# Running sums of the decay: one token-major copy in place of a second, head-major product

## What is computed

```python
a_cs = jnp.cumsum(a_dt, axis=-1)                       # per head, over the chunk's tokens
seg = a_cs[..., :, None] - a_cs[..., None, :]          # token t minus token s
decay = jnp.where(mask, jnp.exp(jnp.where(mask, seg, 0.0)), 0.0)
cb = jnp.einsum("bclgn,bcsgn->bcgls", cm, bm)
y_diag = jnp.einsum("bcgls,bcgrls,bcsgrp->bclgrp", cb, decay, xdt)
decay_to_end = jnp.exp(a_cs[..., -1:] - a_cs)
```

## Time and profile before

| | us |
|---|---|
| median of 3 runs | 2788.34 (2787.91 to 2789.7) |
| profiled execution, its own time | 2790.36 |
| span of that execution | 2788.5 |
| PE busy | 2737.2 |
| DVE busy | 1883.0 |
| ACT busy | 1454.7 |
| POOL busy | 818.0 |

### The profile page before, as it was taken

How to read it: one execution, slowest core, us unless ns; L and a number is a source line. 1 busy time by engine, 2 the same in 40 slices (tenths; PEclk the granted TensorE clock), 3 DMA queues, 4 the chain that set the end, 5 groups by cost and what they waited for, 6 DMA issues and landing times.

```text
span 2788.5 us, 38529 instructions
## 1 busy us (share of the span) xinstructions
PE 2737.2 (98%) x11715; PEld 1768.6 (63%) x11715; DVE 1883.0 (68%) x5154; ACT 1454.7 (52%) x3396; POOL 818.0 (29%) x1368
## 2 busy tenths in 40 slices
PE   8999999999999999999999999997999999999997
PEld 6777677767776777677767776763444444444443
DVE  5776767676767676767676767665666666666665
ACT  2445544454455444544454445434666666666665
POOL 1121112111211121112111111112556555556555
PEclk9999999999999999999999999998999999999999
DMA  7311111111111111111111111156888677778864
GB/s 305 136 64 46 69 67 48 46 69 61 54 46 69 64 51 46 69 59 56 46 69 61 54 46 61 42 199 252 307 291 294 236 274 255 280 258 293 317 215 146
DMA packets 104914, 377.91 MB, mean 136 GB/s; under 512 B 32713, under 2 KB 34642, under 8 KB 94706
## 3 DMA queue, kind: packets, MB, share of 16 engines
q1 hardware_dynamic: 44226, 236.13, 23.1%
q0 software_dynamic: 60480, 139.24, 14.8%
HBM read 326.14 MB, written 123.03 MB: 161 GB/s over the span
## 4 chain that ended last, share of the span: by engine, by line
PE 95%; DMA 2%; DVE 1%; ACT 1%; issue 1%; SPq 0%; POOL 0%; POOLq 0%; DVEq 0%; ACTq 0%
PE PB L367 24%; PE PB L1659 20%; PE PB L378 16%; PE PB L457 12%; PE SS L1678 5%; PE TB L1678 5%; PE YB L457 4%; PE YB L411 2%; DMA arena<-in_w_in 1%; PE SS L420 1%; PE SS L424 1%; PE TB L433 1%; PE YB L1669 1%; PE MB L402 1%; PE YB L515 0%
## 5 line engine op out<-in xcount | busy, mean ns | idle before, releaser
L367 PE MATMUL PB<-arena,hT 128*128 128x512 f32 (+2 forms) x2112 | 728.3, 498 | 1.8 <-ACT xT L590 1.1
L1659 PE MATMUL PB<-arena,hT 128*128 x1296 | 582.5, 592 | 0.0
L367 PEld LDWEIGHTS PB<-arena,hT 128*128 128x128 f32 x2112 | 396.7, 190 | 276.9 <-issue 229.7
L378 PE MATMUL PB<-hT,arena 128*128 128x128 f32 x4224 | 487.5, 276 | 4.7 <-DVE arena L1148 4.6
L378 PEld LDWEIGHTS PB<-hT,arena 128*128 128x128 f32 x4224 | 481.8, 193 | 8.9 <-issue 4.9
L1659 PEld LDWEIGHTS PB<-arena,hT 128*128 128x128 f32 x1296 | 239.9, 190 | 271.2 <-issue 271.2
L1185 POOL TENSOR_SCALAR rs<-sq 128x2 f32<-128x2 f32 (+1 forms) x66 | 14.2, 216 | 1254.7 <-ACT h L750 910.3
L457 PE MATMUL PB<-arena,tT 128*128 128x274 f32 (+1 forms) x1056 | 361.6, 497 | 0.3 <-ACT tT L644 0.3
L457 PEld LDWEIGHTS PB<-arena,tT 128*128 128x128 f32 x1056 | 197.1, 192 | 142.7 <-issue 123.4
L636 ACT ACTIVATE yb<-ycat 32x128 f32<-32x128 f32 x768 | 235.9, 307 | 89.3 <-DVE ycat L933 48.7
L1789 DVE TENSOR_TENSOR gv<-ycat,PB 128x256 f32<-128x256 f32 x81 | 34.1, 421 | 290.1 <-ACT ycat L1741 280.8
(11 more groups left out here) (292 smaller groups left out, 4109.0 us busy)
## 6 DMA issues: line engine op xcount, KB each, us to landing
arena<-in_w_expert SPq DMA_DIRECT2D x32, 2048.0 KB
arena<-in_w_expert SPq DMA_DIRECT2D x32, 1024.0 KB
h_rows<-h SPq DMA_DIRECT2D x34, 512.0 KB, 2.8
x_in<-in_x_rows SPq DMA_DIRECT2D x33, 512.0 KB, 4.4
hT<-in_x_cols SPq DMA_DIRECT2D x33, 512.0 KB, 3.6
x_res<-in_x_rows SPq DMA_DIRECT2D x33, 512.0 KB, 4.2
dec<-running_sums SPq DMA_DIRECT2D x33, 512.0 KB, 3.6
x_rows<-x_res SPq DMA_DIRECT2D x33, 512.0 KB, 2.6
```

Source lines behind the costliest of these rows:

```text
L367: mm = nc.tensor.matmul(out, hT[u][:, k, :], w_group(name)[:, k, :], start=k == 0, stop=k == KD - 1)
L378: mm = nc.tensor.matmul(PB[b][:, c * P:(c + 1) * P], w_block(name, c)[:, k, :], hT[u][:, k, :], start=k == 0, stop=k == KD - 1)
L1659: mm = nc.tensor.matmul(PB[u][:, :], hT[u][:, k, :], arena[:, bass.ds(slot + k * 2 * DE, 2 * DE)], start=k == 0, stop=k == KD - 1)
```

## The change

The second product and ACT's copy go away, and the tensors `sumT`, `sumT_p` with them. SP now stores `e_in[:, 0:H]`, DVE's copy, token by token: 128 rows of 32 bytes. It waits for `acs_out` (DVE's copy) where it waited for `sumT_out` (ACT's copy). The read back spreads the same 4 KB, so in a partition `dec` now holds the 8 heads of token 0, then the 8 heads of token 1, and so on. All later uses go through `dec_h`, a view of the same memory in which the tokens of one head are 8 elements (32 bytes) apart; only ACT's exponential and the expert phase's use still run over it side by side, and the copy of the last token's sums (L848) becomes contiguous. PE's wait for `gated_ready`, which guarded the bank of `sumT_p`, moves to `pe_states`.

```diff
-        dec = sb("dec", [P, H, P])
+        dec = sb("dec", [P, P * H])
+        dec_t = dec[:, :].rearrange("p (t h) -> p t h", h=H)
+        dec_h = dec[:, :].rearrange("p (t h) -> p h t", h=H)
...
-            nc.tensor.matmul(acs_p, tri_s if t == NP else tri, adt[:], start=True, stop=True)
-            after(pe, s["gated_ready"], t)
-            nc.tensor.matmul(sumT_p, adt[:], tri_s if t == NP else tri, start=True, stop=True).then_inc(s["sumT_done"], 1)
+            nc.tensor.matmul(acs_p, tri_s if t == NP else tri, adt[:], start=True, stop=True).then_inc(s["sums_done"], 1)
...
-                mm = nc.tensor.matmul(bank[:, c], dec[:, h, :], xdt[:, c], start=True, stop=True)
+                mm = nc.tensor.matmul(bank[:, c], dec_h[:, h, :], xdt[:, c], start=True, stop=True)
...
             pe.wait_ge(s["state_ready"], t + 1)
-            pe.wait_ge(s["sumT_out"], t + 1)
+            after(pe, s["gated_ready"], t)
...
-        def act_sums(act, t):
-
-            act.wait_ge(s["sumT_done"], t + 1)
-            after(act, sumT_stored, 16 * t)
-            nc.scalar.activation(sumT[:, :], sumT_p, ACT.Copy).then_inc(s["sumT_out"], 1)
-
...
-            nc.scalar.activation(dec[:, :, :], dec[:, :, :], ACT.Exp).then_inc(s["decay_ready"], 1)
+            nc.scalar.activation(dec[:, :], dec[:, :], ACT.Exp).then_inc(s["decay_ready"], 1)
...
-                st.link(V.tensor_copy(e_in[:, H:2 * H].rearrange("p (h a) -> p h a", a=1), dec[:, :, P - 1:P]))
+                st.link(V.tensor_copy(e_in[:, H:2 * H], dec_t[:, P - 1, :]))
...
-                ins = V.tensor_scalar(dec[:, h, :], dec[:, h, :], a, a, ALU.min, ALU.subtract)
+                ins = V.tensor_scalar(dec_h[:, h, :], dec_h[:, h, :], a, a, ALU.min, ALU.subtract)
...
-                ins = V.tensor_tensor(dec[:, half(g), :], dec[:, half(g), :],
+                ins = V.tensor_tensor(dec_h[:, half(g), :], dec_h[:, half(g), :],
                                       cbm[:, g:g + 1, :].broadcast_to([P, 4, P]), ALU.mult)
...
-            sp.wait_ge(s["sumT_out"], t + 1)
-            sp.dma_start(sumT_d, sumT[:, :]).then_inc(sumT_stored, 16)
-            sp.wait_ge(sumT_stored, 16 * (t + 1))
+            sp.wait_ge(s["acs_out"], t + 1)
+            sp.dma_start(sums_d, e_in[:, 0:H]).then_inc(sums_stored, 16)
+            sp.wait_ge(sums_stored, 16 * (t + 1))
             after(sp, s["ydiag_done"], t)
-            sp.dma_start(flat(dec[:, :, :]), sumT_d.rearrange("(a h) t -> a (h t)", a=1).broadcast_to([P, H * P])).then_inc(sums_spread, 16)
+            sp.dma_start(dec[:, :], sums_d.rearrange("(a t) h -> a (t h)", a=1).broadcast_to([P, H * P])).then_inc(sums_spread, 16)
```

More of the change, by code:

```diff
@@ L139, in build @@
         x2_d = nc.dram_tensor("x2_rows", [T + P, D], F32).ap()
-        sumT_d = nc.dram_tensor("running_sums", [H, P], F32).ap()
+        sums_d = nc.dram_tensor("running_sums", [P, H], F32).ap()
         h2_d = nc.dram_tensor("h2_rows", [T + P, D], F32).ap()
@@ L204, in build @@
         lgr = sb("lgr", [P, NR])
-        sumT = sb("sumT", [H, P])
         rinv = sb("rinv", [P, 2])
@@ L254, in build @@
         wow_p = YB[:, 0:KD * NR]
-        sumT_p = SS[0:H, 0, 0:P]
         names = """tail_packed xa_scaled w_scaled eout_a ws_ready wow_full wow_out xsq_ready xr_ready xi_ready rbc_full x_scaled
@@ L261, in build @@
             halo_saved conv_done xc_ready cb_done xc_moved xb_out
-            dt_read lg_read cb_read rank_read dtneg_ready dtexp_ready dtrec_ready dt_ready acs_out sumT_done sumT_out
+            dt_read lg_read cb_read rank_read dtneg_ready dtexp_ready dtrec_ready dt_ready acs_out sums_done
             ein_ready eout_ready seg_done decay_ready dec_ready xw_ready
@@ L281, in build @@
         lists_set, scattered = sem("lists_set"), sem("scattered")
-        sumT_stored, sums_spread = sem("sumT_stored"), sem("sums_spread")
+        sums_stored, sums_spread = sem("sums_stored"), sem("sums_spread")
         x2_stored, h2_stored = sem("x2_stored"), sem("h2_stored")
@@ L530, in pe_sample_states @@
             pe.wait_ge(smp_T, 16)
-            pe.wait_ge(s["sumT_out"], NT)
+            pe.wait_ge(s["gated_ready"], NP)
             for g in range(G):
@@ L735, in act_turn @@
             nc.scalar.activation(gu[:, :], PB[0][:, :], ACT.Gelu_apprx_tanh).then_inc(s["gu_out"], 1)
-            act_sums(act, i + 1)
             act_silu(act, i + 1)
@@ L783, in act_phase1 @@
             act_silu(act, 0)
-            act_sums(act, 0)
             act_front(act, 0)
@@ L832, in dve_front @@
         def dve_front(dve, st, t):
-            dve.wait_ge(s["sumT_done"], t + 1)
+            dve.wait_ge(s["sums_done"], t + 1)
             V.tensor_copy(e_in[:, 0:H], acs_p).then_inc(s["acs_out"], 1)
@@ L844, in dve_front @@
                 ends = cbm[:, 0, 0:H * SB].rearrange("p (h q) -> p h q", h=H)
-                st.link(V.tensor_tensor(ends, dec[:, :, SL - 1::SL], row_s.rearrange("p (a q) -> p a q", a=1).broadcast_to([P, H, SB]), ALU.mult))
+                st.link(V.tensor_tensor(ends, dec_h[:, :, SL - 1::SL], row_s.rearrange("p (a q) -> p a q", a=1).broadcast_to([P, H, SB]), ALU.mult))
                 st.link(V.tensor_reduce(e_in[:, H:2 * H], ends, AX.X, ALU.add))
             else:
-                st.link(V.tensor_copy(e_in[:, H:2 * H].rearrange("p (h a) -> p h a", a=1), dec[:, :, P - 1:P]))
+                st.link(V.tensor_copy(e_in[:, H:2 * H], dec_t[:, P - 1, :]))
             V.tensor_tensor(e_in[:, 2 * H:], e_in[:, H:2 * H], e_in[:, 0:H], ALU.subtract).then_inc(s["ein_ready"], 1)
@@ L1234, in pool_dt @@
             after(pool, s["xw_ready"], t)
-            after(pool, s["sumT_done"], t)
+            after(pool, s["sums_done"], t)
             r, r2, a = dtw[:, 5, :], dtw[:, 6, :], dtw[:, 7, :]
@@ L1405, in build @@
         list_rows = gu[:, 0:2 * P]
-        g_buf = [x_in[0][:, :], x_in[1][:, :], flat(xc[:, :, :]), flat(dec[:, :, :])]
+        g_buf = [x_in[0][:, :], x_in[1][:, :], flat(xc[:, :, :]), dec[:, :]]
         y_buf = [x_res[0][:, :], x_res[1][:, :]]
```

## The result

| | before | after |
|---|---|---|
| median, us | 2787.97 (2786.95 to 2789.7, 6 runs) | 2866.93 (2865.36 to 2868.22, 6 runs) |
| span of the profiled execution | 2788.5 | 2864.9 |
| PE busy | 2737.2 | 2810.3 |
| DVE busy | 1883.0 | 1918.7 |

The changed kernel is slower: ratio 1.0282, 95% interval 1.0271 to 1.0293, 79 us. The forecast was 2832.6 us, with 2842 as the upper end of its range. The direction and the chief cause were right, the size was not: the change cost 79 us where 44 were forecast.

The account below looks back on a forecast made before the run. PE's instructions, one after the other, were taken to bound the kernel. -9.9 (product) + 50.7 (weight loads) + 3.5 (sample tile) = +44.3 us on 2788.3 gave 2832.6 us, 1.6% slower; range 2778 to 2842.

Parts of the forecast that it names:

- What bounds the kernel: Prompt turns cost PE's instructions one after the other; other engines cost nothing until PE waits; PE busy 98% of the span.
- The product that goes: Dropping L395 on PE saves 0.32 us in each of 31 tiles, 9.9 us gained (6.5 at 0.21).
- The weight loads of `pe_ydiag`: L411's loads, reading columns 32 bytes apart, take 207 ns instead of 108; 512 prompt loads cost 50.7 us.
- the upper bound that I kept: If the pace of L411's loads just halves, 108 ns more a load, 55.3 us in all.
- Nearly full clock throughout: Profile reading at the start: PE busy in 98% of the span, at nearly full clock throughout; no cost priced for it.
- VectorE's far work: DVE's strided L852 and L876, 2048 elements a tile, cost 1.2 us more a tile (0 to 2.4), hidden in prompt turns.
- The later start of the store: Store waits for DVE's copy; DVE stands 3.7 us more, hidden from PE in prompt turns with 0.8 us of room.
- The small pieces: The store's 128 pieces of 32 bytes, about 6 ns each, add 0.7 us (0 to 1).
- The sample tile: Later store and strided DVE work lie on the path there: 2.0 to 4.1 us lost, 3.5 taken.
- The first: Rival: PE's far loads do not slow, 0 instead of 50.7; time 2782.0 us, range 2780 to 2786; chance 0.34.
- The second: Rival: DVE becomes what PE waits for; 6.4 us over 16 tighter turns, 2788 us, or 2839 with slow loads; alone 0.05.
- The third: Rival: loads slow by more than twice; at 3 x 108 ns, 110 us more, 2892 us; chance 0.04.

Follow-up runs that it names:

- x4: Kernel before without the second product L395 for tiles 1 to 32, ScalarE copying constants instead (output wrong): 2776.9 us, ratio 0.9959.
- y1: Kernel before, but PE's stationary operand in L411 read with a step of 1 to 8 elements by turn (output wrong): one execution, 2843.4 us.
- x1: Kernel before with only PE's stationary operand of L411 read at a step of 8 elements (output wrong, more expert blocks): 2887.4 us, ratio 1.0358.
- x3: Kernel before with each of the 8 products of L411 made twice, all loads near: 2848.7 us, ratio 1.0214.
- y4: Changed kernel, but in turns 1 to 31 each head's far-load product follows one of the 8 products of projection vb: 2814.1 us, ratio 1.0091 to before.
- x2: Changed kernel, but the spread lands in h2 and VectorE writes dec head by head, so PE's loads are near: 2780.4 us, ratio 0.9969.
- y3: Kernel before, with only SyncE's store of sumT also waiting for VectorE's copy of the sums: 2792.3 us, ratio 1.0012.

## Why the prediction was right and where it failed

- **What bounds the kernel.** Right. PE without gaps in prompt turns, and VectorE's longer wait cost PE nothing there.
- **The product that goes.** Size a little off: 0.39 us a turn, not 0.32 (0.53 less 0.14 in the profile; 0.41 a turn in x4). The step that failed is the sentence that the next load follows after L393 at the pace of its 0.21: with L395 gone, L393 itself goes to the next line in 0.14.
- **The weight loads of `pe_ydiag`.** The mechanism is right, the term was too small: 99 ns a load were forecast, 120 came (228 against 108), 61.1 us and not 50.7. Even the upper bound that I kept, a halved pace at 55.3, lay below it. The working had 1.62 ns for each far element; PE needs 1.78. A part of the miss is in the reading of a row: 1.29 us for 1024 elements is 1.26 ns each and not 1.0 to 1.1, and with 0.59 for the distance the same working gives 1.85 ns, 129 ns more a load and 66 us. So the measured price lies between the two, and a single row of 64 elements on another engine was no measure to 10%. y1 shows that even past 16 bytes the price still moves between 211 and 228 ns.
- **The clock.** This is the step that failed most, and it took the time out of the range: I priced the longer line and held all lines behind it at their old times, so the sum has nothing for them, and they took 24.4 us more. "Nearly full clock throughout" was read as a fact that the change would leave alone. In the changed kernel the granted clock falls to half for 3.4 us in 17 of the 32 turns. x1 shows that the far loads alone bring it, and x3 and y4 that it takes far loads in a row and not only a line of this length. Whether PE's thinner work or the far reads as such are behind it is not shown.
- **VectorE's far work.** 1.2 us a tile forecast, 1.2 measured, but the sum is right by luck: the forecast had 0.6 for each of the two groups, and they took 0.40 and 0.77 more.
- **The later start of the store.** VectorE's wait in the tighter turns 3.7 us forecast, 2.9 to 3.6 measured (3.55 in the turn shown; the 3.77 of x2 is a turn of the other kind). The small pieces cost less than the 0.7 us taken: the store lands in 1.4 us, where the step from one issue to the other was 1.22. Hidden in prompt turns, as forecast (y3).
- **The sample tile.** 2.0 to 4.1 forecast with 3.5 taken; 4.7 measured. The later start alone costs 3.7 (y3), but not as the forecast had it, by waiting: 1.0 is waiting and 2.9 half clock behind the longer wait. That the number came close is partly luck; the clock was missing here too.
- **The rivals.** The first (loads that do not slow) is false, and with it the rule that the prediction took from the Trainium skill, page "TensorE: Matmul & The Clock Gate", section LDWEIGHTS, that a load's time goes by its columns alone; y1 shows 128 columns at 108 to 228 ns. The second (DVE as the bound) is false. The third named three times the 108 ns and is false at 2.1 times.
- **The sum.** With the measured terms, 61.1 - 12.1 + 4.7 = 53.7 would have been at the very edge of the range (2842); with the clock's 24.4, 78.1, it is far outside, and near the 79 measured.

What stays open: what in the far loads brings the clock down, and what decides in which turns it falls. In the changed kernel it is every second tile from tile 4 on, in x1 ten stretches without that order, with the same line of 3.64 us.

## What to carry to other kernels

A stationary operand that PE reads with a step pays as soon as fewer than two columns lie in 16 bytes: a load of 128 float32 columns takes 167 ns with step 3 and 211 to 228 from step 4 on, and not 108. Let the engine that has time change the layout: VectorE read far and wrote near for 1.2 us a tile that nobody waited for in prompt turns, and so turned a loss of 79 us into a gain of 9; the price is a second buffer. When a change slows a row of PE's loads for a few microseconds, or makes PE wait that long, reckon with half clock for the lines behind it as well, and look at the granted clock of the stretches, not of the whole.

## What the runs showed of the hardware that I had not expected

- The granted clock fell to 1.2 GHz for 3.4 us at the end of 3.64 us of far loads, in 17 of 32 turns, and never in 3.52 us of near ones with twice the products (x3), though PE is busy without a gap in both.
- Steps of 5 and 6 elements (211 and 212 ns a load) are a little cheaper than 4 and 8 (223 and 228 ns).
- A store of 128 pieces of 32 bytes landed in 1.4 us.
